# Every second bank of turned probabilities emptied by ScalarE, and the sample's exponential moved one step ahead, in a hybrid decoder kernel on one core

## The reference, cut to what matters

```python
s = jnp.einsum('znqhd,znkhd->znhqk', qb, kc) * (Dh ** -0.5)
...
m = jnp.max(s, axis=-1, keepdims=True)
p = jnp.exp(s - m)
den = jnp.sum(p, axis=-1)
o = jnp.einsum('znhqk,znkhd->znqhd', p, vc) / den.transpose(0, 1, 3, 2)[..., None]
```

## Time and profile before

| | |
|---|---|
| median of 3 runs | 2945.09 us (2944.14 to 2949.34) |
| the profiled execution, its own time | 2940.5 us |
| its span, first to last instruction | 2938.5 us |
| TensorE, busy share of the span | 97% |
| attention stage | from about 1553 to 2037 us of the span |
| mean granted TensorE clock | 0.997 of full |

### The profile page before, as it was taken

One profiled execution on the slowest core, in us unless ns is written; L12 is line 12 of the kernel. 1 busy time (PEld: TensorE's weight loads), 2 busy tenths in 40 slices (PEclk: granted clock), 3 DMA queues, 4 the chain that ended last, 5 costly groups with the idle time before them and its releaser, 6 DMA issues.

```text
span 2938.5 us, 47540 instructions
## 1 busy us (share of the span) xinstructions
PE 2857.0 (97%) x21361; PEld 2720.3 (93%) x21361; DVE 1351.0 (46%) x1749; ACT 784.1 (27%) x1238; POOL 138.9 (5%) x225
## 2 busy tenths in 40 slices
PE   6999999999999999999998999998999999999999
PEld 6999999999999999899996776777999999999999
DVE  5754543444444444635503655556444444444444
ACT  5444522111111111322214444544221111111111
POOL 1010000000000000200011111110000000000000
PEclk9999999999999999999999999999999999999999
DMA  5120211111111111132248657763111111111111
GB/s 190 44 66 18 105 58 44 44 43 44 44 43 44 44 44 43 58 111 79 80 164 257 213 195 245 247 207 127 58 44 43 44 44 44 43 43 44 43 44 61
DMA packets 126250, 253.80 MB, mean 86 GB/s; under 512 B 7586, under 2 KB 88694, under 8 KB 125537
## 3 DMA queue, kind: packets, MB, share of 16 engines
q1 hardware_dynamic: 112960, 189.29, 20.0%
q0 software_dynamic: 11776, 56.96, 5.7%
q10 hardware_dynamic: 1312, 4.52, 0.4%
HBM read 222.72 MB, written 28.02 MB: 85 GB/s over the span
## 4 chain that ended last, share of the span: by engine, by line
PE 90%; DVE 3%; ACT 3%; DMA 2%; POOL 1%; SPq 1%; issue 1%; ACTq 0%; POOLq 0%; DVEq 0%
PE psum L223 63%; PE psum L459 13%; PE psum L1855 3%; PE psum L1912 2%; PE psum L1870 2%; PE psum L1834 2%; PE psum L1883 1%; ACT smp_kt L1966 1%; DMA cache_tile<-in_cache_k 1%; POOL prep_sq L297 1%; SPq L1805 1%; DMA x_natural<-in_x_prompt 1%; DVE att_pt L2037 0%; PE psum L568 0%; ACT att_scores L1983 0%
## 5 line engine op out<-in xcount | busy, mean ns | idle before, releaser
L223 PE MATMUL psum<-h_hi,w_hi 128*128 128x364 f32 (+1 forms) x2592 | 574.9, 330 | 6.6 <-DVE h_lo L289 5.7
L223 PE MATMUL psum<-h_lo,w_hi 128*128 128x364 f32 (+1 forms) x2592 | 571.4, 328 | 0.0
L223 PE MATMUL psum<-h_hi,w_lo 128*128 128x364 f32 (+1 forms) x2592 | 568.6, 328 | 0.0
L223 PEld LDWEIGHTS psum<-h_hi,w_hi 128*128 128x128 f32 x2592 | 448.6, 188 | 10.1 <-issue 6.9
L223 PEld LDWEIGHTS psum<-h_lo,w_hi 128*128 128x128 f32 x2592 | 449.1, 188 | 0.0
L223 PEld LDWEIGHTS psum<-h_hi,w_lo 128*128 128x128 f32 x2592 | 448.7, 188 | 0.0
L205 ACT ACTIVATE w_hi<-w_raw 128x2048 fp32r<-128x2048 f32 x96 | 183.7, 1914 | 665.3 <-PE psum L223 609.2
L459 PE MATMUL psum<-w_hi,h_hi 128*128 128x256 f32 (+1 forms) x1152 | 326.8, 284 | 2.2 <-DVE h_lo L289 2.2
L459 PE MATMUL psum<-w_hi,h_lo 128*128 128x256 f32 (+1 forms) x1152 | 324.2, 281 | 0.0
L459 PE MATMUL psum<-w_lo,h_hi 128*128 128x256 f32 (+1 forms) x1152 | 323.6, 281 | 0.0
L1473 DVE TENSOR_TENSOR x_res<-x_res,psum 128x1092 f32<-128x1092 f32 x176 | 227.4, 1292 | 200.2 <-PE psum L223 200.2
(11 more groups left out here) (310 smaller groups left out, 3199.3 us busy)
## 6 DMA issues: line engine op xcount, KB each, us to landing
cache_tile<-in_cache_k SPq DMA_DIRECT2D x64, 512.0 KB, 8.2
cache_tile<-in_cache_v SPq DMA_DIRECT2D x64, 512.0 KB, 6.6
w_raw<-in_w_ffn_gate SPq DMA_DIRECT2D x22, 1024.0 KB, 5.1
w_raw<-in_w_ffn_up SPq DMA_DIRECT2D x22, 1024.0 KB, 5.1
w_raw<-in_w_ffn_down SPq DMA_DIRECT2D x22, 1024.0 KB, 4.9
w_raw<-in_w_in_att SPq DMA_DIRECT2D x12, 1024.0 KB, 7.1
w_raw<-in_w_in_rec SPq DMA_DIRECT2D x10, 1024.0 KB, 5.0
park_x<-x_res POOLq DMA_DIRECT2D x2, 4368.0 KB, 13.1
```

The lines of the kernel that those rows point to most:

```text
L223: mm = pe.matmul(PS[:, bank + c, 0:n], st[:, slot, wc:wc + P], mv[:, k, c * CW:c * CW + n], start=(i < NCH), stop=(i >= 3 * NCH * nk - NCH))
```

## The change

Three things in the attention stage. Of the prompt's turned banks, those with c = 4 and c = 12 are copied to `att_pt` by ScalarE instead of VectorE (64 of 160: 48 of 128x512 and 16 of 128x256), at the places that ScalarE's own turns have; `pv` waits for the last two takes instead of the last one, since they now lie on two engines. The sample's exponential stands at the end of s = 5, after ScalarE's turns and ahead of L2010, instead of in s = 6 after the first two turns. And at s = 6 the three turns of the sample come ahead of the prompt's turn instead of behind it.

```diff
         if n == NSLOT - LEAD + 2:
             units += [("out", 0, 0), ("out", 1, 0)]
+        if s == 6:
+            units += [("s", b, z) for z in range(3)]
         if 1 <= n <= NSLOT:
             units += [("p", n - 1, k) for k in range(0, 2 * ((n - 1) % QT + 1), 4)]
-        if s == 6:
-            units += [("s", b, z) for z in range(3)]
         return units
+
+    def by_act(unit):
+        what, x, c = unit
+        return c % 8 == 4 if what == "p" else what != "s"
...
+    def last_turns(n, what, x):
+
+        gs = [T0[n] + i for i, u in enumerate(turns(n)) if u[0] == what and u[1] == x]
+        return [(g % 2, g // 2 + 1) for g in gs[-2:]]
...
-            bank, count = last_turn(m + 1, "p", m)
-            pe.wait_ge(t_out[bank], count)
+            for bank, count in last_turns(m + 1, "p", m):
+                pe.wait_ge(t_out[bank], count)
...
+            elif what == "p":
+                k = min(4, 2 * (x % QT + 1) - c)
+                act.activation(PT[:, x % 2, c:c + k, :].rearrange("p a w -> p (a w)"), bank[:, 0:k * P],
+                               ACT.Copy).then_inc(t_out[g % 2], 1)
...
-            mine = [i for i, u in enumerate(turns(n)) if u[0] not in ("p", "s")]
+            mine = [i for i, u in enumerate(turns(n)) if by_act(u)]
             for i in mine[0:2]:
                 take(n, i)
-            if s == 6:
-                act.wait_ge(b_mn, b + 1)
-                act.activation(SS[:, :], SS[:, :], ACT.Exp, bias=NMN[:, 0:1], scale=-1.0,
-                               accum_out=DNS[:, 0:1]).then_inc(b_p, 1)
             if 0 <= n < NSLOT:
                 probs(n, 0)
...
             for i in mine[3:]:
                 take(n, i)
+            if s == 5:
+                act.wait_ge(b_mn, b + 1)
+                act.activation(SS[:, :], SS[:, :], ACT.Exp, bias=NMN[:, 0:1], scale=-1.0,
+                               accum_out=DNS[:, 0:1]).then_inc(b_p, 1)
...
-                    if units[i][0] in ("qk", "p", "s"):
+                    if units[i][0] == "qk" or not by_act(units[i]):
                         take(n, i)
```

## The result

The change makes the kernel slower: 2956.95 us median of 8 runs (2951.77 to 2958.53), against 2946.81 us (2943.52 to 2949.34) for the kernel before in 8 runs; the ratio is 1.0032, with a 95% interval of 1.0023 to 1.0041, so 9.4 us (6.8 to 12.1); the medians are 10.1 us apart. The sum had been +8.9 us. (The runs had a median of 2945.09 for the kernel before when the prediction was made; with more of them it is 2946.8 to 2947.7.)

What follows compares the result with a forecast made beforehand. TensorE was taken to bound the kernel, so only its waits count. Takes 0, samples +4.3 and last steps +4.6 summed to +8.9 us on a median of 2945.1, forecasting 2954.0 us, range 2946 to 2964.

Steps and rivals of the forecast that it cites:

- Bound and place: Whole kernel: TensorE, busy 97% of the span, bounds it; time can change only where it waits, in the attention stage.
- The takes, 0 us: Before step 59: moving bank copies from VectorE to ScalarE alone is worth 0 us.
- bounds of -1.1 and +1: Moved takes before step 59: at best 12 waits shorter by 0.094 us, -1.1 us; at worst +1 us.
- The exponential, +1.1 us of waiting, +0.8 net a sample: End of s = 5: L2010 behind the exponential delays att_out and pv 1.1 us; net +0.8 us in six samples.
- -0.1 and -0.5: First and last sample: small gains in us instead of the loss of the six samples between.
- The turns' order: At s = 6: the prompt's turn fills part of the wait for the sample's bank, giving back 0.3 us a sample.
- The last steps, +4.6 us: Steps 59 to 65: ScalarE's prompt takes stand ahead of both exponentials and delay the last tile; bounds 0 and +7 us.
- Faster: Rival: the takes' waits go and pv is not held up, at most 13.8 us, 2931.3 us; chance 0.06.
- Same: Rival: the s = 6 delay is hidden by the cache-tile wait, leaving the last steps' +4.6, 2949.7 us; chance 0.22.
- The rival of the clock: Rival: each new wait of 1.1 us lowers TensorE's clock, some 1.5 us seven times, +10.5, 2964.5 us; chance 0.07.

Runs made afterwards that it cites:

- the mended kernel: The change with the exponential behind att_rden_rows and VectorE alone taking the prompt's tiles 58 to 63; 2946.56 us against 2947.27 for the kernel before, ratio 0.9999.
- e1: The change, with the sample's exponential behind att_rden_rows in s = 5 instead of ahead of it; 2951.04 us against 2947.74 for the kernel before, ratio 1.0009.
- e5: The kernel before, with only the sample's three turns put ahead of the prompt's in s = 6; 2946.83 us against 2947.27, ratio 1.0001.
- e3: The kernel before, with only the banks c = 4 and c = 12 taken by ScalarE; 2950.9 us against 2947.74, ratio 1.0012.
- e2: The kernel before, with only the exponential moved to the end of s = 5, ahead of att_rden_rows; 2957.23 us against 2947.74, ratio 1.0029.
- e4: The change, but the prompt's tiles 58 to 63 taken by VectorE alone; 2951.61 us against 2947.74 for the kernel before, ratio 1.0011.

## Why the prediction was right, point by point

**Bound and place.** Right: all but the end's last term lies in the attention stage. TensorE reaches the stage's end, the first L223, at 2053.4 instead of 2036.8, with the clock's share and the 1.5 us from ahead of the stage in it.

**The takes, 0 us.** Right as far as the runs can tell: the mended kernel with and without them is the same (0.2 us between the medians, and TensorE's waits for other engines 31.1 and 30.7 us). The times alone do not show the bounds of -1.1 and +1. The argument that a sum of work on engines that are not full decides nothing was what the experiments bore out.

**The exponential, +1.1 us of waiting, +0.8 net a sample.** Right in mechanism, place and size. Predicted on the timeline were `pv` 1.1 us late and the weighing 0.8; the trace has 1.12 and 0.90. `att_rden_rows` came 4.0 us later against the queries' turn next to it, as said. That six samples have the wait and the first and the last do not was right too. For those the sum had -0.1 and -0.5 us. In the first, from the scores of its step s = 6 to the weighing, it was 6.48 us before (1581.29 to 1587.77) and is 6.31 now (1582.74 to 1589.05), -0.17. From the last sample's scores to its weighing it was 7.14 us before (1986.96 to 1994.10) and is 6.55 now (1998.32 to 2004.87), -0.59.

**The turns' order.** The share given back was a little mis-sized: 0.3 us a sample by the prediction, 0.22 in the change, 0.21 in `e1`, and 0.12 when done alone. The wait of 0.35 us for the first bank's copy is not the reason, since the predicted timeline had it. In `e5` it is the exponential: `pv` starts at 1761.51, the exponential's sum is read by 1763.61, and the sample's first turn starts at 1763.76, 2.25 us after `pv` where the change has 2.11 (1762.02 to 1764.13). The same 2.24 to 2.25 us stand in the other five of the six samples: with the old place of the exponential this order waits for it a little each time.

**The last steps, +4.6 us.** The sum was about right, two of its terms were not. Held: +0.35 at `smp_out_twice` (1.31 for 0.96; I had 0.5), +2.25 for the two exponentials behind the fourth take (2.5 predicted), and about 0.9 later on in the projection, where 1.1 was predicted: its first block of L223 takes 95.6 us instead of 94.7 (from the first to the last matmul of `att_hi` and `w_hi`), 95.5 and 95.6 in `e1` and `e3`, and 94.7 to 94.8 in `e2` and `e4`, which have no takes there. The step that failed is "in steps 61 and 62 L2010, VectorE's weight split and with it the minima of step 63 come later: +0.35". They came no later: from the turns of step 61 to those of step 63 it is 8.34 us in both kernels, and the minima of step 63 start 1.5 us after those in both. ScalarE's copy was indeed late, but `att_out` in step 62 has VectorE's own copy of a bank ahead of it (to 2034.02 in the trace after, against 2033.78 for the end of ScalarE's). I had followed the queue of one engine and not of the other. In its place came the low clock, 1 to 1.7 us, which I had put only in the bounds. So 0.35 + 2.25 + 0.9 + 1 to 1.7 is 4.5 to 5.2 us; that it came out near 4.6 is luck to the extent of this exchange. By `e3`, the end is worth 3.5 us (0.9 to 5.9), by `e4` against the change 6.2, uncertain by more than 3 us.

**The rivals.** Faster failed as its own counter-argument had it: `smp_pt` and `att_pt` together still cost 8.6 us of 11.5. The rule of the Trainium skill that goes with it (VectorE: DVE Perf Modes, Specifications: ScalarE sits closer to PSUM) holds in the durations, 594 ns against 689 ns a bank, and said nothing on the time. Same failed as expected: the wait for the cache tile of the third sample did not shrink with the delay (1.41 us at 1777.97, before 1.32), so the tile came later along with the weighing. The rival of the clock was wrong for the waits within the samples and half right for the end. For the rule of the Trainium skill beside it (TensorE: Matmul & The Clock Gate, A second HAM failure mode), that frequent micro-idles made the clock of a kernel go down and up again, the repeats of the kernel before are the better case: low stretches do turn up in a stage full of short waits, 17 us of them, and beyond the first sample at different places in each run.

## What to carry to other kernels

On an engine that works in the order issued, as ScalarE's rows show here, put work that somebody waits for soon ahead of work that nobody waits for soon; here exchanging a 0.27 us copy and a 1.37 us exponential decides over some 6.7 us. When work moves to an engine with time to spare, look at what is queued behind it there at each place where it lands, the edges of the loop included: a rule such as "the first two of my turns" gave the takes a harmless place in the steps up to 58 and one ahead of everything in the last six. And if an engine's time in a stage falls by 30 us and the waits that end on it hardly change, expect nothing: here the medians with and without were 0.2 us apart.

## What the runs showed that I had not expected

The time at the 1.2 GHz level in one stage varied between 3.4 and 17 us over three profiles of the same kernel, which were up to 9 us apart. TensorE's waits for the other engines hardly differed, but those for cache tiles came to 7.3, 10.6 and 10.7 us. At most 6.9 us for the clock (half of 13.8, an estimate) and 3.3 for the tiles cover the difference. A comparison of two single profiles would have put the loss at 17 us; the medians have 10.
